# The first query/key projection in the wide form, and the first probability map left unscaled

## What is computed

```
q, k, v = split(h @ w_qkv)                      # 8 heads, two maps of width 64 each, v of width 128
s = einsum(q, k) * 64 ** -0.5 - slope * |i - j|
a = softmax(s)
a = a[0] - lam * a[1]                           # two probability maps of a head
o = rmsnorm(a @ v, subln, eps=1e-5) * (1 - 0.2)
out = o @ w_o
```

## Time and profile before

| | |
|---|---|
| median of 3 runs | 1223.0 us (1222.5 to 1223.69) |
| the profiled execution | 1226.66 us, its span 1224.8 us |
| TensorE busy | 1216.0 us (99% of the span) |
| VectorE busy | 965.6 us (79%) |
| ScalarE busy | 701.7 us (57%) |
| GpSimd busy | 77.5 us (6%) |
| chain that ended last | TensorE 95%, VectorE 2%, ScalarE 1%, DMA 1% |

### The profile page before, as it was taken

The page is one execution under the profiler, slowest core; times in us unless marked ns, Lnnn a source line. Parts: engine busy times, 40 slices in busy tenths (PEclk is TensorE's granted clock), DMA queues, the critical chain, the costliest instruction groups (busy, mean ns, idle before and its releaser), DMA issues.

```text
span 1224.8 us, 20310 instructions
## 1 busy us (share of the span) xinstructions
PE 1216.0 (99%) x7638; PEld 1086.4 (89%) x7638; DVE 965.6 (79%) x1325; ACT 701.7 (57%) x1029; POOL 77.5 (6%) x97
## 2 busy tenths in 40 slices
PE   9999999999999999999999999999999999999998
PEld 7999888888988898888899998888888889888886
DVE  6997887766688878777567988999767887899943
ACT  6576655544657665555446446766545776666642
POOL 0001000032000000000000100000300500000000
PEclk9999999999999999999999999999999999999999
DMA  8535587655455457765555666776565634777551
GB/s 300 179 133 138 151 246 224 207 177 200 166 191 170 139 138 212 197 183 189 178 188 170 213 188 197 200 204 191 182 201 155 208 116 129 221 197 198 189 190 50
DMA packets 277586, 223.70 MB, mean 183 GB/s; under 512 B 8360, under 2 KB 264624, under 8 KB 277264
## 3 DMA queue, kind: packets, MB, share of 16 engines
q1 hardware_dynamic: 275200, 214.44, 57.6%
q0 software_dynamic: 1744, 7.78, 1.8%
q10 hardware_dynamic: 576, 0.57, 0.1%
HBM read 221.71 MB, written 1.06 MB: 182 GB/s over the span
## 4 chain that ended last, share of the span: by engine, by line
PE 95%; DVE 2%; ACT 1%; DMA 1%; issue 0%; ACTq 0%; POOLq 0%; POOL 0%
PE ps L1935 36%; PE ps L1941 19%; PE ps L1812 6%; PE ps L1813 6%; PE ps L1814 6%; PE ps L1908 4%; PE ps L1913 2%; PE ps L2185 2%; PE ps L2063 2%; PE ps L2065 2%; PE ps L2064 2%; PE ps L2151 2%; PE ps L2149 2%; PE ps L2150 2%; PE ps L2204 1%; PE ps L2238 1%
## 5 line engine op out<-in xcount | busy, mean ns | idle before, releaser
L1057 DVE TENSOR_TENSOR wlo<-raw,whi 128x2048 fp32r<-128x2048 f32 x187 | 422.5, 2261 | 101.3 <-ACT whi L665 101.1
L665 ACT CAST whi<-raw 128x2048 fp32r<-128x2048 f32 (+1 forms) x203 | 382.1, 1883 | 133.7 <-PE ps L1814 48.6
L1935 PE MATMUL ps<-x,whi 128*128 128x512 f32 x1408 | 337.4, 391 | 0.0
L1935 PEld LDWEIGHTS ps<-x,whi 128*128 128x128 f32 x1408 | 258.1, 188 | 49.3
L1812 PE MATMUL ps<-x,whi 128*128 128x256 f32 x680 | 196.6, 289 | 0.2 <-DVE wlo L1057 0.2
L1813 PE MATMUL ps<-x,whi 128*128 128x256 f32 x680 | 192.2, 283 | 0.0
L1814 PE MATMUL ps<-x,wlo 128*128 128x256 f32 x680 | 192.2, 283 | 0.0
L1941 PEld LDWEIGHTS ps<-x,wlo 128*128 128x128 f32 x1408 | 180.8, 191 | 7.4
L1941 PE MATMUL ps<-x,wlo 128*128 128x256 f32 x1408 | 183.2, 283 | 0.0
L1812 PEld LDWEIGHTS ps<-x,whi 128*128 128x128 f32 x680 | 129.7, 191 | 2.7 <-issue 1.1
L1813 PEld LDWEIGHTS ps<-x,whi 128*128 128x128 f32 x680 | 129.8, 191 | 0.3
(11 more groups left out here) (205 smaller groups left out, 1479.8 us busy)
## 6 DMA issues: line engine op xcount, KB each, us to landing
raw<-in_ffn_w_in SPq DMA_DIRECT2D x88, 512.0 KB, 4.9
raw<-in_ffn_w_gate SPq DMA_DIRECT2D x44, 512.0 KB, 3.9
raw<-in_ffn_w_up SPq DMA_DIRECT2D x44, 512.0 KB, 5.2
raw<-in_ffn_w_out SPq DMA_DIRECT2D x38, 512.0 KB, 4.0
raw<-in_ffn_w_down SPq DMA_DIRECT2D x32, 512.0 KB, 4.4
raw<-in_na_w_qkv SPq DMA_DIRECT2D x24, 512.0 KB, 4.2
raw<-in_od_w_in SPq DMA_DIRECT2D x24, 512.0 KB, 4.6
raw<-in_da_w_qkv SPq DMA_DIRECT2D x22, 512.0 KB, 5.2
```

The source lines that it names most:

```text
L665: nc.scalar.copy(whi[:, c % RING, 0:n], raw[:, c % RING, 0:n]).then_inc(w_hi, 1)
L1057: nc.vector.tensor_tensor(wlo[:, c % RING, 0:n], raw[:, c % RING, 0:n], whi[:, c % RING, 0:n].bitcast(F32), ALU.subtract).then_inc(w_lo, 1)
L1935: return mm(bank(banks[f]), hi[:, k, cols[f]], x[:, k, :, :].rearrange("p a t -> p (a t)"), start=first, stop=end, skip_group_check=opened ...
```

## The change

The first attention's projection goes over to the wide form, with the bank pairs (0, 1) and (2, 3) in turn. TensorE's list loses one matmul a block. ScalarE's copy takes the second halves only. VectorE gets `add_halves` at the very end of its odd steps, behind `norm_o`. TensorE now waits for two value copies at step 2, since chunk 1 uses banks 2 and 3, and from chunk 2 on for the halves of the chunk two before.

`normalise` no longer scales the first map. One reciprocal serves both maps; the second map's factor becomes -lambda times the first sum over the second, so that the combined map is too large by the first sum, and the square (ScalarE, scale) and the head norm (VectorE, second scalar) multiply by the first reciprocal.

```
-WO_BANKS = {"wo0": (0, 2, 1, 3), "wo1": (0, 1, 2, 3), "wo3": (0, 1, 2, 3)}
+WO_BANKS = {"wo0": (0, 1, 2, 3), "wo1": (0, 1, 2, 3), "wo3": (0, 1, 2, 3)}
...
                 b0 = 2 * (i % 2)
-                if name == "qk3":
+                if name != "qk1":
                     nc.scalar.activation(qkT[:, at:at + 2, :], ps[:, b0:b0 + 2, S:2 * S], ACT.Copy,
                                          scale=scale).then_inc(qk_half, 1)
...
                         ins = nc.scalar.activation(osq[:, t, :], bank(7)[:, t * P:(t + 1) * P],
-                                                   ACT.Square, accum_out=ostat[:, 0, j, t:t + 1])
+                                                   ACT.Square, scale=rsum[:, 2 * j, t:t + 1],
+                                                   accum_out=ostat[:, 0, j, t:t + 1])
...
                 def normalise(u):
                     ve.wait_ge(exp_ok, base + u + 1)
-                    link(nc.vector.reciprocal(rsum[:, u, :], sums[:, u, :]))
                     if a == 0:
-                        if u % 2 == 0:
-                            return
-                        link(nc.vector.tensor_scalar(rsum[:, u, :], rsum[:, u, :], tiny[:, 4:5],
-                                                     None, ALU.mult))
-                        for t in range(TT):
-                            off, n = span(a, t)
-                            p0 = prob[:, (u - 1) % 4, off:off + n]
-                            ins = nc.vector.tensor_scalar(p0, p0, rsum[:, u - 1, t:t + 1], None,
-                                                          ALU.mult)
-                        link(ins)
+                        link(nc.vector.reciprocal(rsum[:, u - 1:u + 1, :], sums[:, u - 1:u + 1, :]))
+                        link(nc.vector.scalar_tensor_tensor(
+                            out=rsum[:, u, :], in0=rsum[:, u, :], scalar=tiny[:, 4:5],
+                            in1=sums[:, u - 1, :], op0=ALU.mult, op1=ALU.mult))
...
                         ins = nc.vector.tensor_scalar(onrm[:, t, :], bank(7)[:, t * P:(t + 1) * P],
-                                                      ostat[:, 2, j, t:t + 1], None, ALU.mult)
+                                                      ostat[:, 2, j, t:t + 1], rsum[:, 2 * j, t:t + 1],
+                                                      ALU.mult, ALU.mult)
...
                     if a == 0 and 0 <= j < PAIRS:
-                        normalise(2 * j)
                         normalise(2 * j + 1)
                     if a == 0 and 0 <= j - 1 < PAIRS:
                         norm_o(j - 1)
+                    if a == 0 and s < 16:
+                        add_halves(s // 2)
...
-                    if s == 2 and a:
+                    if s == 2:
                         pe.wait_ge(v_ok, 4 * a + 2)
...
-                        if s % 2 == 0 and i >= RING:
-                            pe.wait_ge(copied, COPY_BASE[qk] + i - RING + 1)
-                        if s == 0:
-                            f_both(QK_BANKS[0], START[qk], x,
-                                   lambda k: pe.wait_ge(xn_lo, 4 * a + k // 2 + 1))
-                        elif s > 1:
-                            f_tile(QK_BANKS[i % 3], START[qk] + i, s % 2, x, between)
+                        if s % 2 == 0 and i >= 2:
+                            pe.wait_ge(copied, COPY_BASE[qk] + i - 1)
+                        if a < 2 and s == 0:
+                            wide_both((0, 1), START[qk], x,
+                                      lambda k: pe.wait_ge(xn_lo, 4 * a + k // 2 + 1))
+                        elif a == 2 or s > 1:
+                            wide_tile(2 * (i % 2) + s % 2, START[qk] + i, s % 2, x, between)
```

More of the change, by code:

```diff
@@ L130 @@
 V_BANKS = ((2, 3, 5, 7), (2, 3, 5, 7), (2, 3, 5, 7))
-QK_BANKS = (0, 1, 2)
-WO_BANKS = {"wo0": (0, 2, 1, 3), "wo1": (0, 1, 2, 3), "wo3": (0, 1, 2, 3)}
+WO_BANKS = {"wo0": (0, 1, 2, 3), "wo1": (0, 1, 2, 3), "wo3": (0, 1, 2, 3)}
 PROJ_BANKS = (2, 3, 5, 6)
@@ L1388, in normalise @@
                     else:
+                        link(nc.vector.reciprocal(rsum[:, u, :], sums[:, u, :]))
                         for t in range(TT):
@@ L1429, in add_halves @@
                 def add_halves(i):
-                    ve.wait_ge(qk_half, 8 * (a - 1) + i + 1)
+                    ve.wait_ge(qk_half, 8 * a + i + 1)
                     at, b0 = qk_tile(qk, i), 2 * (i % 2)
@@ L1814, in three @@
                 return mm(dst, lo, x[:, 0, :], start=False, stop=stop)
[L1816 to L1826, removed]
             def f_tile(b, c, f, x, between=None, turn=0):
@@ L2300, in attention @@
                         i = s // 2
[L2301 to L2305, removed]
-                                          lambda k: pe.wait_ge(xn_lo, 4 * a + k // 2 + 1))
-                            elif a == 2 or s > 1:
-                                wide_tile(2 * (i % 2) + s % 2, START[qk] + i, s % 2, x, between)
-                            continue
-                        if s % 2 == 0 and i >= RING:
-                            pe.wait_ge(copied, COPY_BASE[qk] + i - RING + 1)
-                        if s == 0:
-                            f_both(QK_BANKS[0], START[qk], x,
-                                   lambda k: pe.wait_ge(xn_lo, 4 * a + k // 2 + 1))
-                        elif s > 1:
-                            f_tile(QK_BANKS[i % 3], START[qk] + i, s % 2, x, between)
+                        if s % 2 == 0 and i >= 2:
[5 more added lines that the diff above has]
+                            wide_tile(2 * (i % 2) + s % 2, START[qk] + i, s % 2, x, between)
                     else:
```

## The result

The changed kernel takes 1225.69 us (median of 13 runs, 1225.21 to 1226.64) against 1222.96 us of the kernel before; the ratio is 1.0023, with a 95% interval of 1.0016 to 1.0030. That is 2.7 us slower, where 1.4 us slower was forecast. The interval leaves out no change; the 0.23% lies just above the 0.2% that the prediction took for the least that can be told from no change.

The account below looks back on a forecast made before the run. TensorE's issue order was taken to bound the first attention; -1.4 (wide projection) + 0.8 (second chunk's bank) + 2.0 (scores behind the head norm) = +1.4 us on 1223.0, so 1224.4 us, range 1222.1 to 1226.4.

Parts of the forecast that it names:

- What bounds the kernel: First attention, 60 to 90 us: TensorE, busy 30.00 of 30 us, sets the end by its issue order.
- The projection in the wide form: First attention's query/key projection: 2.79 instead of 2.875 us a tile, so TensorE gains 1.4 us in all.
- New wait one: Ahead of the second chunk: TensorE waits 0.8 us for VectorE's value copies to release the bank.
- New wait two: Scores of pairs 2, 4, 6 wait for halves added behind the head norm: 0.45, 0.45, 1.1, together 2.0 us.
- the chain: From TensorE's product with v through square, GpSimd, head norm and halves to the scores: 4.2 us.
- rival two: GpSimd's two steps each wait for a VectorE combination in three chains: +2.4 us, so 1226.8; chance 0.16.
- the row that I weighed at 94.16: GpSimd's power ran 0.70 us while an undelayed VectorE combination started at 94.32; cited against GpSimd and VectorE colliding.
- VectorE's lap: VectorE's two-pair lap, waits included: 16.6 us, just under TensorE's 16.7, so no bound on the order.
- Rival one: Scores never wait, since the chain is quicker or the halves come in time: -0.6 us, 1222.4; chance 0.12.
- Rival three: In the wide projection, matmul durations count instead of starts: 22 us gained, 1201; chance 0.04.
- the forecast's own: Range 1223.3 to 1225.4 us, from scores' waits of 0.9 to 3.0 us; chance 0.68.
- signs of being wrong: VectorE without idle time in 60 to 90 us, GpSimd steps over 0.4, or a tile distance other than 2.79.

Follow-up runs that it names:

- e6: The kernel before with only the unscaled map (changed `normalise`, square and head norm), projection left plain: 1223.30 us, ratio 1.0001.
- e7: The edits of e3, and VectorE adds the halves of chunk 1 ahead of the split in step 3: 1221.71 us, ratio 0.9990.
- e2: The changed kernel with the first attention's values in banks 3, 5, 6, 7 instead of 2, 3, 5, 7: 1224.92 us, ratio 1.0016.
- e3: The changed kernel with halves ahead of the head norm and values in banks 3, 5, 6, 7: 1221.98 us, ratio 0.9993.
- e1: The changed kernel with VectorE adding the halves ahead of the head norm instead of behind it: 1222.55 us, ratio 0.9995.
- e4: The changed kernel with the first sum's reciprocal left out of the square and the head norm: 1224.46 us, ratio 1.0013.
- e8: The edits of e3 (halves ahead of the head norm, other value banks) on e5: 1225.94 us, ratio 1.0025.
- e5: The changed kernel with the old normalisation (two reciprocals, first map scaled, no factors), halves behind the head norm: 1229.12 us, ratio 1.0049.

## Why the prediction held, and which terms were mis-sized

**What bounds the kernel** was right. TensorE's issue order did, and e6 shows the other side: less work for VectorE alone is worth nothing in the kernel before.

**The projection in the wide form.** The forecast was 1.4 us; without waits (e7) the stage is 91.42 - 90.31 = 1.1 us shorter. The undisturbed tile is 2.79 us as read, but a lap fell from 17.03 only to 16.78 and not to 16.7: 0.06 a tile, not 0.085. By the starts in the two traces, the tiles of that lap take 11.96 us in e7 and 12.23 before, 0.27 less where four undisturbed tiles give 0.34; the loss is spread over the seven places where other work cuts in. By the estimate from the Trainium skill's fixed cost (TensorE: Matmul & The Clock Gate, "Wait — 56ns, not 53.3ns?") the gain would have been 0.3; the measured 1.1 is nearer to the rows.

**New wait one** was right in size and in kind. TensorE was idle from 34.60 + 2 x 0.23 = 35.06 to 35.79, 0.73 us, where 0.8 was forecast, and e2 took it out. What the prediction didn't say is that the first scores had only 0.3 us left over, so that without this wait 0.23 of it comes back there (e2, e3), until the halves move (e7).

**New wait two** is the term that was too small. It was placed rightly, and TensorE's own arrival was right to 0.06 us (e1). Against that arrival the waits were 59.72 - 54.91 - 3.77 = 1.04, then 0.67 and 1.31, together 3.0 us; 2.0 were forecast. Two prices were wrong. The first: I took the reciprocal as a scalar of operations that stay, at nothing, with up to 0.1 us each as a bound that I then left out of the chain. By line, the kernel before:

```profile
L797 ACT ACTIVATE osq<-ps x16: 268/274/278, 59.0 to 117.7; 128x128 f32<-128x128 f32 x16
...
L1402 DVE TENSOR_SCALAR onrm<-ps,ostat x16: 336/342/351, 61.4 to 119.5; 128x128 f32<-128x128 f32 x16
```

and the changed one (ns min/median/max):

```profile
L791 ACT ACTIVATE osq<-ps,rsum x16: 358/364/369, 56.0 to 116.6; 128x128 f32<-128x128 f32 x16
...
L1391 DVE TENSOR_SCALAR onrm<-ps,ostat,rsum x16: 398/404/411, 58.3 to 118.5; 128x128 f32<-128x128 f32 x16
```

That is 0.09 and 0.06 us each, two of each in a chain: 0.3 us on three waits, 0.9 us. e4 gave back 1.2, of which 0.2 is GpSimd's steps at pair 0 being shorter there. Both prices lie within the bound that I named; they belonged into the sum, since every one of them stood on the path. At pair 4 the chain was only 4.44 - 4.23 = 0.21 longer than forecast, since the forecast's chain had a first GpSimd step of 0.32 in it and here it took 0.19.
The second, at one of the three chains: GpSimd's steps were longer there. GpSimd and VectorE at pair 0's norm in the changed kernel:

```profile
56.90 0.47 POOL L583 TENSOR_SCALAR ostat<-ostat 128x2 f32<-128x2 f32 x1 [33.17 <-ACT osq L791]
57.45 0.86 POOL L585 TENSOR_TENSOR ostat<-ostat,half 128x2 f32<-128x2 f32 x1
```

```profile
56.83 0.88 DVE L1373 SCALAR_TENSOR_TENSOR prob<-prob,rsum 128x256 f32<-128x256 f32 x2
```

They take 0.47 and 0.86 beside VectorE's combination, and 0.19 and 0.76 at pair 2, which makes 0.38 us; with three times 0.21 that is the 1.0 us by which the term was too small. It would be rival two's mechanism, at part of its price and at one chain. The Trainium skill (SBUF — State Buffer, "Who interferes with whom") calls the port that VectorE and GpSimd share an exclusive lock. The first step here, which began 0.07 after a combination's start, was 0.28 longer than usual, in keeping with that, and so it was in e1 and e3 (0.47 and 0.48); the row that I weighed at 94.16 was not. Nor is e2, where the step began 0.04 after a combination's start and was not longer:

```profile
56.92 0.19 POOL L583 TENSOR_SCALAR ostat<-ostat 128x2 f32<-128x2 f32 x1 [32.59 <-ACT osq L791]
57.20 0.79 POOL L585 TENSOR_TENSOR ostat<-ostat,half 128x2 f32<-128x2 f32 x1
```

```profile
56.88 0.91 DVE L1373 SCALAR_TENSOR_TENSOR prob<-prob,rsum 128x256 f32<-128x256 f32 x2
```

So what makes the steps longer stays open. What they cost is shown: in e2 they are 0.35 us shorter together, and the wait ahead of pair 2's scores is 0.36 shorter.

**VectorE's lap** was too short in the forecast: 16.6 us, just under TensorE's 16.7. Without the 0.59 us for GpSimd the lap of the changed kernel is 17.44 - 0.59 = 16.85, a little above TensorE's 16.78. So the chain did set the lap, as forecast, but VectorE's load behind the head norm would have set it too, if only by 0.07. With the halves ahead of the norm, VectorE's wait for the scores is 0.70 where VectorE is the bound (e8) and no longer 1.22, so the swap of e1 also takes the load down to about 15.6 + 0.7 = 16.3 a lap. VectorE's work alone, without any wait, is 17.44 - 0.59 - 1.22 = 15.6 us a lap (15.3 forecast), and 18.21 - 1.22 = 17.0 without the unscaled map (e5), which is above 16.78 wherever the halves stand: e5 and e8 have laps of 18.2 and 17.7. So the two halves of the change belong together: the wide form brings VectorE the halves, and the unscaled map pays for them.

**The rivals and the sum.** Rival one did not occur in the changed kernel, and e1 is the kernel in which it does: 1222.55 against the 1222.4 worked out. Rival three is ruled out by the tile distance. The forecast's sum with the measured terms is -1.1 + 0.7 + 3.0 = +2.6 us, and the stage shows 2.61. The time of 1225.69 lies inside the range of 1222.1 to 1226.4, but outside the forecast's own, 1223.3 to 1225.4: the scores' waits were at its upper end of 3.0, and the wide form brought 0.3 less than its term, to which the range gave no width. It is in the range because half of rival two was taken in. It is slower by a little more than 0.2%, where within 0.2% had been given 0.80 and slower 0.16. Of the signs of being wrong one came, at one place: a first GpSimd step of 0.47 us, over 0.4.

## What to carry to other kernels

A step that releases another engine should not stand in a queue behind a step that waits for a third one: the same 0.69 us of added halves cost 3 us behind the head norm and nothing ahead of it. When an engine is close to being the bound, look for the place where it waits for the one that sets the end, and put the releasing step in front of such a wait. A factor that is read from a tile, in place of a constant or as a second one, was not free here (0.06 to 0.09 us an operation); find its price wherever the operation stands on a path between two engines.

## What the runs showed of the hardware that was not expected

Two operations became longer by one more per-partition scalar: ScalarE's square of 128x128 from PSUM, from 274 to 364 ns with its scale read from a tile, and VectorE's 128x128 scaling from PSUM, from 342 to 404 ns with a second such factor. The same two operations take 362 and 402 ns in e6, whose projection is plain, and 274 and 344 in e4, where only the factors are gone. An idle time of 2.02 us of TensorE in e5 was followed by a granted clock of 0.62 and 0.52 in the next two stretches of 2 us (the lower of its two levels, 1.2 GHz, for most of them). In the same execution idle times of 1.21 and 1.39 us left it at 1.00, as the 1.24 us did in the changed kernel from 90 to 120 us:

```profile
90.00:120.00 30.00, 28.76 (x239) 27.51 (x238) 21.48 (x36) 18.67 (x45) 3.62 (x8) 1.00 0.50 137
```
